# One 512 KB load, one ring slot and one semaphore per half unit of raw weights, in place of 1 MB loads of two half units

## The reference, cut to what matters

```
x = x + 0.5 * rmsnorm(swiglu(rmsnorm(x, g[0]), ffn_w_in[i, 0], ffn_w_out[i, 0]), g[1])
x = x + rmsnorm(mixer(rmsnorm(x, g[2])), g[3])
x = x + 0.5 * rmsnorm(swiglu(rmsnorm(x, g[4]), ffn_w_in[i, 1], ffn_w_out[i, 1]), g[5])
gate = jax.nn.sigmoid(rmsnorm(x, g[6]) @ ple_w_gate[i])
x = x + rmsnorm(gate * (p[i] @ ple_w_proj[i]), g[7])
```

## Time and profile before

| what | value |
|---|---|
| time, median of 3 runs | 1773.73 us (1773.48 to 1776.33) |
| span of the profiled execution, first to last instruction | 1774.4 us |
| TensorE busy (matmul) | 1715.8 us, 97% |
| VectorE busy | 1088.8 us, 61% |
| ScalarE busy | 883.9 us, 50% |
| mean TensorE clock granted | 0.991 of full speed |
| HBM read | 298.08 MB, with writes 169 GB/s over the span |
| DMA engines, share of the main queue | 47.3% |

### The profile page before, as it was taken

The page is one execution under the profiler, slowest core; times in us unless marked ns, Lnnn a source line. Parts: engine busy times, 40 slices in busy tenths (PEclk is TensorE's granted clock), DMA queues, the critical chain, the costliest instruction groups (busy, mean ns, idle before and its releaser), DMA issues.

```text
span 1774.4 us, 28208 instructions
## 1 busy us (share of the span) xinstructions
PE 1715.8 (97%) x11992; PEld 1572.3 (89%) x11992; DVE 1088.8 (61%) x1420; ACT 883.9 (50%) x1373; POOL 175.3 (10%) x192
## 2 busy tenths in 40 slices
PE   9999999999998999999989999999999999999996
PEld 8899799899986998989889997799999888899995
DVE  5455667677777544668665556655556686655555
ACT  5344556544566455453554445544445445544444
POOL 0000001209002002920010000100000000000001
PEclk9999999999999999999999999999999999999998
DMA  6655443554554444540545554465445323455552
GB/s 232 242 190 190 165 159 129 178 192 172 190 190 166 178 167 143 190 143 25 178 160 190 189 183 175 168 219 197 176 182 177 143 96 104 170 197 190 183 193 76
DMA packets 51086, 300.99 MB, mean 170 GB/s; under 512 B 6073, under 2 KB 12689, under 8 KB 17169
## 3 DMA queue, kind: packets, MB, share of 16 engines
q1 hardware_dynamic: 50800, 298.66, 47.3%
q0 software_dynamic: 160, 0.52, 0.1%
HBM read 298.08 MB, written 1.09 MB: 169 GB/s over the span
## 4 chain that ended last, share of the span: by engine, by line
PE 75%; DVE 8%; ACT 8%; DMA 4%; issue 2%; POOL 1%; SPq 1%; DVEq 0%; POOLq 0%; ACTq 0%
PE PS L1860 72%; DVE wlo L1147 3%; DMA raw<-in_w 3%; ACT whi L661 3%; PE PS L1863 2%; ACT wk L704 1%; DVE xn L1236 1%; ACT SC L795 1%; POOL st L551 1%; DMA SC<-in_pT 1%; ACT SC L883 1%; PE PS L2000 1%; ACT xn L716 0%; PE PS L2182 0%; DVE X L1228 0%
## 5 line engine op out<-in xcount | busy, mean ns | idle before, releaser
L1147 DVE TENSOR_TENSOR wlo<-raw,whi 128x1024 fp32r<-128x1024 f32 x528 | 659.5, 1257 | 441.3 <-ACT whi L661 440.4
L661 ACT ACTIVATE whi<-raw 128x1024 fp32r<-128x1024 f32 x528 | 551.3, 1054 | 416.8 <-PE PS L1860 236.7
L1860 PE MATMUL PS<-xhi,whi 128*128 128x256 f32 x2520 | 716.3, 285 | 4.1 <-DVE wlo L1147 3.2
L1860 PE MATMUL PS<-xhi,wlo 128*128 128x256 f32 x2520 | 710.7, 283 | 0.0
L1860 PE MATMUL PS<-xlo,whi 128*128 128x256 f32 x2520 | 704.6, 283 | 0.0
L1860 PEld LDWEIGHTS PS<-xhi,whi 128*128 128x128 f32 x2520 | 482.9, 192 | 12.2 <-DVE wlo L1147 4.5
L1860 PEld LDWEIGHTS PS<-xhi,wlo 128*128 128x128 f32 x2520 | 483.0, 192 | 0.0
L1860 PEld LDWEIGHTS PS<-xlo,whi 128*128 128x128 f32 x2520 | 479.6, 192 | 2.1
L1860 PE MATMUL PS<-whi,hhi 128*128 128x512 f32 x544 | 175.1, 396 | 5.0 <-DVE wlo L1147 5.0
L1860 PE MATMUL PS<-wlo,hhi 128*128 128x512 f32 x544 | 172.9, 392 | 0.0
L1860 PE MATMUL PS<-whi,hlo 128*128 128x512 f32 x544 | 172.6, 391 | 0.0
(11 more groups left out here) (267 smaller groups left out, 1465.8 us busy)
## 6 DMA issues: line engine op xcount, KB each, us to landing
raw<-in_w SPq DMA_DIRECT2D x264, 1024.0 KB, 4.8
gr<-in_rows SPq DMA_DIRECT2D x23, 512.0 KB, 3.8
SC<-scratch SPq DMA_DIRECT2D x1, 2048.0 KB, 10.6
SC<-scratch SPq DMA_DIRECT2D x2, 1024.0 KB, 11.0
X<-in_x SPq DMA_DIRECT2D x2, 512.0 KB, 4.1
xn<-in_sc SPq DMA_DIRECT2D x2, 512.0 KB, 6.1
out<-xn SPq DMA_DIRECT2D x2, 512.0 KB, 2.6
SC<-in_pT SPq DMA_DIRECT2D x3, 256.0 KB, 4.0
```

What stands on the lines that cost most here:

```text
L661: a.activation(whi[:, u % NSPLIT, :], raw[:, u // 2 % NRAW, u % 2 * HU:u % 2 * HU + HU], ACT.Copy).then_inc(s_hi, 1)
L1147: v.tensor_tensor(wlo[:, u % NSPLIT, :], src, hi.bitcast(f32), SUB).then_inc(s_lo, 1)
L1860: return pe.matmul(o, l, r, start=start, stop=stop)
```

## The change

The ring `raw` has four slots of 512 KB in place of two of 1 MB, the same memory. Each half unit has its own DMA, which waits for the split of the half unit four before it. The bound of `weights(v)` is written in half units: with v even the last half unit issued by a call was v + 7 and is now v + 6; with v odd it was and is v + 6. ScalarE waits for the semaphore of each half unit's slot. The data read and the arithmetic are the same.

```
-NRAW = 2
+NRAW = 4
...
-        raw = sb("raw", [128, NRAW, U])
+        raw = sb("raw", [128, NRAW, HU])
...
-                while at[0] <= min((v + AHEAD - 1) // 2 + NRAW, N_HALF // 2 - 1):
+                while at[0] <= min(max(v + AHEAD - 1, -1) + NRAW, N_HALF - 1):
                     u = at[0]
                     at[0] += 1
                     if u >= NRAW:
-                        q.wait_ge(s_lo, 2 * (u - NRAW) + 2)
-                    sp.dma_start(raw[:, u % NRAW, :], w[u]).then_inc(s_raw[u % NRAW], 16)
+                        q.wait_ge(s_lo, u - NRAW + 1)
+                    sp.dma_start(raw[:, u % NRAW, :], w[u // 2][:, u % 2 * HU:u % 2 * HU + HU]).then_inc(s_raw[u % NRAW], 16)
...
-                    q.wait_ge(s_raw[u // 2 % NRAW], 16 * (u // 2 // NRAW + 1))
+                    q.wait_ge(s_raw[u % NRAW], 16 * (u // NRAW + 1))
                     if u >= NSPLIT:
                         q.wait_ge(s_used, u - NSPLIT + 1)
-                    a.activation(whi[:, u % NSPLIT, :], raw[:, u // 2 % NRAW, u % 2 * HU:u % 2 * HU + HU], ACT.Copy).then_inc(s_hi, 1)
+                    a.activation(whi[:, u % NSPLIT, :], raw[:, u % NRAW, :], ACT.Copy).then_inc(s_hi, 1)
...
-                    src = raw[:, u // 2 % NRAW, u % 2 * HU:u % 2 * HU + HU]
+                    src = raw[:, u % NRAW, :]
```

## The result

The changed kernel takes 1782.91 us (median of 5 runs, 1781.56 to 1783.57), the kernel before beside it 1774.72 us (1773.48 to 1776.54). The ratio is 1.0047, 95% interval 1.0034 to 1.006: 8 us slower. The forecast was 1783.9 us.

A forecast was written before the change was run, and what follows sets the result against it. TensorE, busy 97% of the span, was taken as the bound. Steady flow -0.8, bias_out -7.3 and two gate stalls with low clock +18.3 gave 1784.6 us against the profiled span, 1783.9 as median; range 1769 to 1791.

The forecast's parts named there:

- the sum: Whole kernel: 1774.4 - 0.8 - 7.3 + 18.3 = 1784.6 us against the profiled span, 1783.9 as median, 0.6% slower.
- raw loads were to land in 3.3 to 4.2 us: Sign named for the profile after: landing time of raw loads; above 5 us in steady flow would mean slow half loads.
- 264 more issues: SyncE's queue: 264 added issues of 0.328 us, together 87 us, fit under its 1451 us of waiting and cost nothing.
- Steady flow: Half units in a slot's first half load 2.87 us earlier, removing small TensorE waits: -0.8 us (0 to -2).
- bias_out: First feed-forward part: scratch loads issue 5.7 us earlier, TensorE's 4.27 us stall and low clock go: -7.3 us (-3 to -7.3).
- The gate after settle 3: Half unit 169 goes out behind the row waiting for the norm; TensorE stalls 5.6 us (4.3 to 6.9).
- the clock: Low clock behind each of the two gate stalls: 3.0 us each, +6.0 us in all (0 to 6).
- The gate after settle 7: The same late load in settle 7, landing in 5.9 us: TensorE stalls 6.7 us (4.6 to 8.3).
- one half unit less ahead is harmless outside the gate: Other stages use half units one by one, want LAST + 6 over 10 us after the norm; the load is hidden.
- The third PLE part: SyncE has no more rows to wait for there: no effect and no new TensorE wait.
- Size of the DMAs: 512 KB loads in place of 1 MB: no charge, since loads overlap and TensorE asks for 512 KB only every 3.36 us.

## Why the prediction was right, point by point

The sign, the place and the mechanism of the forecast stand; the sum was 10.2 us above the median of before, the measured difference is 8.2 (8.3 by the ratio, 6.0 to 10.6). Between the two profiles it is 6.5, 3.7 less than the sum: the gates cost 14.1 us and not 18.3, and 0.6 us came in elsewhere. Of the signs named ahead, one failed outright: raw loads were to land in 3.3 to 4.2 us, and the median is 4.4.

- **264 more issues cost nothing.** SyncE still waits over 1300 us for splits (the view of its queue gives 1334.9, 501 times). Half-size DMAs alone were not slower.
- **Steady flow, -0.8 us.** The waits at 519.21 and 523.34 are gone. The table has 2.9 us outside bias_out, 1.1 ahead of it and 1.8 between settles 1 and 3; some of it is shorter waits for a norm, so not all is the work of the change.
- **bias_out, -7.3 us.** Forecast: scratch loads near 49.2, SyncE free near 61.5, half unit 19 in at 66.8 and a stall of nothing to 1 us. Measured: 48.14, 61.59, 67.49 and 1.80 us, without low clock behind it. TensorE, 1.1 us ahead by then, wanted 19 at 68.06 and not at 69.1. The gain in the table is 5.4 us, not 7.3. That both gains together, put at 8.1 us, are 8.25 at the mark of 533.31 is luck: one was put too high and the other too low by about as much. Why the gain comes was right in the main point, the time between the scratch issue and the want; that it needs the half loads was not said, and it doesn't.
- **The gate after settle 3, 5.6 us and 3.0 for the clock.** Landing of 169: forecast 5.1 us, measured 5.2 (537.70 - 532.52). Without the stall the fourth part would have started at 542.69 - 8.25 = 534.44; it started at 540.07, 5.6 us later. The rest of the 7.02 us is 1.4, the low clock.
- **The gate after settle 7, 6.7 and 3.0.** Landing 5.9 us (1107.74 - 1101.88), as forecast. 1105.38 - 1.58 = 1103.80, start at 1110.11: 6.3 us. The rest of the 7.12 us is 0.8, and that is two things: from the start of the fourth part to the next settle the changed kernel takes 24.81 us, just as after settle 3 (540.07 to 564.88), so the low clock costs about 1.4 us again; and the kernel before lost some 0.6 us there on other waits (0.79 us for a norm at 1126.56) that the changed kernel does not have.
- **The term that was mis-sized most is the clock.** I counted 3.0 us for each, as after the stall of the earlier trace rows; it was about 1.4 for each. Windows of the changed kernel (stretch, its us, busy us of five engines, granted clock, DMA share, GB/s):

```profile
533.00:535.20 2.20, 1.89 (x4) 1.16 (x4) 0.25 (x1) 0.00 (x0) 0.00 (x0) 0.50 0.67 209
535.40:540.00 4.60, 0.00 (x0) 0.00 (x0) 1.21 (x2) 2.03 (x3) 0.00 (x0) 0.50 1.00 393
540.00:542.00 2.00, 1.93 (x5) 1.55 (x6) 1.21 (x3) 0.00 (x0) 0.00 (x0) 0.50 0.64 246
542.00:544.00 2.00, 2.00 (x8) 1.62 (x7) 0.00 (x0) 0.00 (x0) 0.00 (x0) 0.72 0.47 162
```

- The granted clock was at 0.50, the 1.2 GHz level, already from 533, in the small gaps ahead of the stall, where before it was 1.00; so most of the low spell fell into the time in which TensorE stood anyway, and over 542 to 544 the granted clock is 0.72. At settle 7 it is the same: 0.73 over 1102 to 1104, ahead of the stall, 0.50 through it, and 0.71 over 1112 to 1114. A low spell costs only what TensorE would have done in it.
- **Not foreseen, +0.9 us:** the third pT load, slowed by the half loads issued right behind it (TensorE's wait is 1.35 us there against 0.49). I had written that one half unit less ahead is harmless outside the gate; it is, for the weights, but the loads that are held come out beside a transfer that is waited for.
- **The third PLE part: nothing**, as said; no new wait there.
- **Size of the DMAs: nothing**, as said. The Trainium skill (DMA: Bandwidth & Descriptors, Rules for kernel authors) wants 1 MiB per DMA for full bandwidth. Here 512 KB loads landed in 4.4 us against 4.8 for 1 MB, and the same bytes kept the DMA engines busy 52.5% of the span against 47.3%. So the rule's direction agrees with the trace, and its price is hidden: TensorE asks for 512 KB only every 3.4 us, and half-size DMAs alone gave a ratio of 0.998. The fit in the same page's section on the anatomy of one DMA, which is for GpSimd-issued ones, gives 3.2 us for 512 KB as an estimate; the measured 4.4 decides.

## What to carry to other kernels

When loads are made finer, write down for every place where the issuing queue blocks which is the last load ahead of it, before and after: an index rounded to whole units hides one load more than the same index in half units. Then look for the one stage that wants that load early, which is where a group of several loads is used at once. The long list of waits on a helper engine (180 us here) is no gain to be had; the wait on the bound engine (12 us) is, and it can grow while the other shrinks.

## What the runs showed of the hardware that I had not expected

- Half the bytes in a load save little: landing 4.4 us in place of 4.8 (median of 528 and 264), while the row loads of the same 512 KB took 3.8 to 4.0.
- Loads issued later delay an earlier one that is still under way: ScalarE's wait for the third pT load was 2.99 us in the kernel before, where the next raw load went out only after it had landed, 3.86 with half loads issued 0.5 us behind it, and 3.26 with SyncE made to wait. Over all profiles it is 3.86 to 4.09 us in the four with half loads right behind it and 2.99 to 3.27 in the seven without. At the two other pT loads no clear difference showed.
- Issuing can block for long: the DMA right behind the scratch loads (3 MB in pieces of 1 KB and 512 B) took 5.7 us to issue, whether it was the lam load of 128 KB (5.73, and 6.99 with the scratch loads one unit earlier) or a raw load of 512 KB (5.72, after which the lam load took 0.44). A raw load takes 0.33 us otherwise (median). That the many small pieces are the reason was not tested.
- A spell of low clock does not need the long stall, and it is not in every run: in the profile of the changed kernel with the bound of before, which has no stall in this gate, the granted clock was 0.50 from 534 to 536 with TensorE busy all the time; in the kernel before it was 1.00 at the same place in the program, with the same two gaps in front (about 1.8 and 0.5 us). Over 15 runs of the kernel before, one and the same program, the mean granted clock lies between 0.990 and 0.995.
